# Modulation products moved from the softmax loop into the projection, head norm moved into the loop, recurrence norm split in two halves

## The reference, cut to what matters

```python
mod = silu(c) @ w_mod + b_mod                    # 6144 columns: six vectors of 1024
sh1, sc1, gt1, sh2, sc2, gt2 = split(mod, 6)
h = rmsnorm(x, g_pre_mix) * (1 + sc1) + sh1
parts = h @ w_in
# differential attention, 4 heads, 128 queries at a time
s = einsum(q, k_all) * scale                     # two maps m = 0, 1 of 1280 keys
pr = softmax(s)
o = (pr[0] - lam * pr[1]) @ v_all
y_d = rmsnorm(o, subln_w, 1e-5) * (1 - lam_init)     # over the 128 columns of a head
# recurrence
rw = dwconv(parts[..., :RWKV_COLS], rwkv_conv)
y = scan(forward) + scan(backward)
yn = (y - mean(y)) * rsqrt(var(y) + 64e-5) * ln_x_w + ln_x_b   # over the 64 columns of a head
y_r = (yn + bonus) * (sigmoid(gl) @ g2)
out = concat(y_r, y_d) @ w_out
x = x + gt1 * rmsnorm(out, g_post_mix)
h = rmsnorm(x, g_pre_ffn) * (1 + sc2) + sh2
```

## Time and profile before

| | us |
|---|---|
| median of 3 runs (3825.49 to 3829.32) | 3826.44 |
| the profiled execution | 3825.82 |
| its span (first to last instruction) | 3824.1 |
| TensorE busy in the span | 3526.0 (92%) |
| VectorE busy | 1891.0 (49%) |
| ScalarE busy | 936.4 (24%) |
| mean granted TensorE clock | 0.958 |

### The profile page before, as it was taken

The page is one execution under the profiler, slowest core; times in us unless marked ns, Lnnn a source line. Parts: engine busy times, 40 slices in busy tenths (PEclk is TensorE's granted clock), DMA queues, the critical chain, the costliest instruction groups (busy, mean ns, idle before and its releaser), DMA issues.

```text
span 3824.1 us, 63573 instructions
## 1 busy us (share of the span) xinstructions
PE 3526.0 (92%) x28813; PEld 2216.9 (58%) x28813; DVE 1891.0 (49%) x2735; ACT 936.4 (24%) x1856; POOL 47.2 (1%) x114
## 2 busy tenths in 40 slices
PE   7998879989999999498999989999899799999988
PEld 3446655559989888244444434445566445777753
DVE  2038852245555564435555550023999663444524
ACT  3015630125455554121000000000011301233310
POOL 2000000000000000000000000000000000000000
PEclk9999989989999999699999999999899899999999
DMA  6011110000000000213111121113011112010021
GB/s 224 22 44 67 67 66 7 28 6 18 4 17 4 4 4 6 94 55 105 66 61 44 42 77 41 50 55 94 22 33 39 39 67 62 22 34 23 1 81 62
DMA packets 110625, 177.53 MB, mean 46 GB/s; under 512 B 5379, under 2 KB 66562, under 8 KB 109714
## 3 DMA queue, kind: packets, MB, share of 16 engines
q1 hardware_dynamic: 101074, 139.49, 10.9%
q10 hardware_dynamic: 9280, 33.97, 2.4%
HBM read 147.23 MB, written 26.21 MB: 45 GB/s over the span
## 4 chain that ended last, share of the span: by engine, by line
PE 84%; DVE 9%; ACT 4%; DMA 2%; issue 1%; ACTq 0%; SPq 0%; DVEq 0%; POOL 0%; POOLq 0%
PE psum_all L66 82%; ACT sbuf_all L75 3%; DVE sbuf_all L94 3%; DVE sbuf_all L84 3%; DVE sbuf_all L102 3%; PE psum_all L69 2%; ACT L75 1%; DMA sbuf_all<-in_w_mod 1%; DMA sbuf_all<-in_w_out 1%; DVE sbuf_all L91 0%; DMA sbuf_all<-in_gla_w_out 0%; DVE sbuf_all L90 0%; DVE sbuf_all L108 0%; DMA sbuf_all<-in_w_down 0%; DVE sbuf_all L97 0%
## 5 line engine op out<-in xcount | busy, mean ns | idle before, releaser
L66 PE MATMUL psum_all<-sbuf_all 64*64 64x64 f32 (+11 forms) x28042 | 3419.2, 307 | 230.9 <-DVE sbuf_all L84 60.0
L66 PEld LDWEIGHTS psum_all<-sbuf_all 64*64 64x64 f32 (+5 forms) x28042 | 2124.9, 153 | 1503.5 <-issue 1066.0
L75 ACT ACTIVATE sbuf_all<-psum_all 128x512 f32<-128x512 f32 (+5 forms) x925 | 408.4, 461 | 1587.7 <-PE psum_all L66 1430.0
L94 DVE SCALAR_TENSOR_TENSOR sbuf_all<-sbuf_all 128x1040 f32<-128x1040 f32 (+8 forms) x571 | 624.1, 1094 | 24.8 <-PE psum_all L66 4.5
L84 DVE TENSOR_TENSOR sbuf_all<-sbuf_all 128x1024 f32<-128x1024 f32 (+9 forms) x589 | 469.7, 821 | 164.4 <-ACT sbuf_all L75 123.2
L75 ACT ACTIVATE sbuf_all<-sbuf_all 128x64 f32<-128x64 f32 (+12 forms) x449 | 259.9, 589 | 895.3 <-DVE sbuf_all L78 396.1
L78 DVE COPY sbuf_all<-psum_all 128x256 f32<-128x256 f32 (+5 forms) x137 | 71.2, 527 | 542.8 <-PE psum_all L66 529.0
L75 ACT ACTIVATE sbuf_all<-psum_all,sbuf_all 128x1280 f32<-128x1280 f32 (+5 forms) x212 | 164.3, 781 | 355.4 <-PE psum_all L66 325.1
L84 DVE TENSOR_TENSOR sbuf_all<-sbuf_all,psum_all 128x512 f32<-128x512 f32 (+3 forms) x160 | 102.0, 640 | 275.9 <-PE psum_all L66 274.8
L108 DVE COPY_PREDICATED sbuf_all<-sbuf_all,psum_all 128x256 f32<-128x256 int32 (+2 forms) x296 | 145.6, 493 | 159.0 <-PE psum_all L66 154.4
L69 PE MATMUL psum_all<-sbuf_all 128*128 128x128 f32 (+2 forms) x771 | 115.7, 295 | 55.9 <-DVE sbuf_all L90 27.1
(11 more groups left out here) (19 smaller groups left out, 125.7 us busy)
## 6 DMA issues: line engine op xcount, KB each, us to landing
sbuf_all<-in_w_mod SPq DMA_DIRECT2D x12, 2048.0 KB, 8.4
sbuf_all<-in_w_up SPq DMA_DIRECT2D x22, 1024.0 KB, 7.6
sbuf_all<-in_w_in SPq DMA_DIRECT2D x6, 2048.0 KB, 7.8
x_spill<-sbuf_all SPq DMA_DIRECT2D x16, 512.0 KB, 2.9
sbuf_all<-in_conv_w_in SPq DMA_DIRECT2D x16, 512.0 KB, 6.3
sbuf_all<-in_gla_w_in SPq DMA_DIRECT2D x8, 1024.0 KB, 5.3
sbuf_all<-in_w_down SPq DMA_DIRECT2D x4, 1792.0 KB, 7.5
hid_spill<-sbuf_all ACTq DMA_DIRECT2D x9, 512.0 KB, 2.6
```

The source lines that it names most:

```text
L66: return self.e.matmul(out, lhsT, rhs, start=start, stop=stop, skip_group_check=True)
L75: return self.e.activation(out, in_, func, bias=bias, scale=scale, **kw)
L94: return self.e.scalar_tensor_tensor(out, a, s, b, op0, op1) if self.e is not None else Unissued()
```

## The change

- The eight modulation blocks leave the softmax loop. In project, VectorE makes all eight products of one block after each of the first eight convolutions, into a `mod_acc` of its own, and TensorE sums each block a step later (steps 1 to 8), in a bank of the common ring. Project's weights use two slots (`rw_blocks`), the modulation one (`mod_blocks`), with the order of loads written out in `project_sync`.
- The norm and turning of head h move into the loop: turns 2 to 6 of the head after it, by the steps `head_mean`, `head_root`, `head_rows`, `turn_out`, `head_out`. Head 3 stays behind the loop.
- Lambda's matmul follows the first scores, and its exponential no longer holds the scores.
- Scanout is made by halves of positions (`scanout_norm`, `scanout_squares`, `scanout_turn`, `scanout_gated`). The second half is done inside mix: VectorE norms it after the gate row and the first half's gates; TensorE turns it ahead of the third block.
- `load_yd` and the `w_out` loads are issued from SP's queue, the first as soon as the scan ends, the others after the gate matmuls and GpSimd's product.

```diff
@@ softmax_tensor
+        if n == 0:
+            te.wait_ge(*A.v.by("lam_products"))
+            bank = open_bank(K, te, "lam", ring=K.small)
+            te.matmul(bank[:, 0:2], K.ones, K.lam[:, 0:2]).then_inc(*A.t.tick("lam"))
...
-        if n and n % 4 == 0 and n <= len(WORK):
-            mod_sum(3 + n // 4)
...
+        if n >= 12 and n % 8 in (4, 5):
+            turn_out(n // 8 - 1, n % 8 - 4)
+    for g in range(2):
+        turn_out(3, g)
@@ softmax_vector
         if n:
             combine(n - 1)
-        if n and n % 4 == 0:
-            mod_sum(3 + n // 4)
+        if h >= 0 and step in (5, 6):
+            head_out(h, step - 5)
         if n < len(WORK):
             top(n, 0)
             top(n, 1)
         if n:
             turned(n - 1, 8)
-        if n < len(WORK):
-            mod_rest(n)
+        if h >= 0 and step == 2:
+            head_mean(h)
+        if h >= 0 and step in (3, 4):
+            head_rows(h, step - 3)
+    head_mean(3)
+    for g in range(2):
+        head_rows(3, g)
+    for g in range(2):
+        head_out(3, g)
@@ softmax_scalar
+        if n >= 10 and n % 8 == 2:
+            head_root(n // 8 - 1)
+    head_root(3)
@@ project_tensor
+        if 1 <= n <= 8:
+            mod_sum(3 + n)
@@ project_vector
+        if 2 <= n <= 9:
+            mod_sum(2 + n)
+        if n < 8:
+            mod_products(4 + n)
@@ project_sync
+    inputs(("rw", 0), 0, RW)
+    inputs(("rw", 1), RW, RW)
+    for block in range(4, 8):
+        modulation(block)
+    inputs(("rw", 2), 2 * RW, RW)
+    for block in range(8, 12):
+        modulation(block)
+    inputs(("lowrank",), 3 * RW, 2 * LORA + GATE)
@@ mix_tensor
-    for s in K.scanout.ends():
-        te.wait_ge(*s)
     gate_row_tensor(K, te, M, "row1", K.mix_diag)
     te.wait_ge(*K.dma("load_yd").final())
     halves = [open_block(K, te, ("out", n), 512) for n in range(2)]
     for i in range(NT):
+        if i == 2:
+            scanout_turn(K, te, 1)
+        te.wait_ge(*K.scanout.v.by("gated", i // 4))
@@ mix_vector
-    for s in K.scanout.ends():
-        ve.wait_ge(*s)
+    ve.wait_ge(*K.scanout.t.by("gate", 1, 3))
     gate_row_vector(K, ve, M, "row1", K.mix_diag, K.mod[:, 16:24], K.col["g_post_mix"])
...
+    scanout_gated(K, ve, 0)
+    scanout_norm(K, ve, 1)
     for i in range(NT):
+        if i == 1:
+            scanout_gated(K, ve, 1)
@@ mix_scalar
+    gate_row_scalar(K, se, M, "row1", K.row1)
+    scanout_squares(K, se, 1)
@@ mix_sync
+    for s in (*K.scan.ends(), K.dma("spill_yd").final()):
         sy.wait_ge(*s)
+    sy.dma_start(K.ydT2, K.yd_dram).then_inc(*K.dma("load_yd").tick())
+    sy.wait_ge(*K.scanout.t.by("gate", 1, 3))
+    sy.wait_ge(*K.scanout.g.by("bonus"))
```

255 lines of the change are left out of this document (134 added, 121 removed).

## The result

The changed kernel takes 3776.28 us (median of 4 runs, 3774.14 to 3779.57), the kernel before 3825.97 (4 runs, 3824.03 to 3829.32): ratio 0.987, 95% interval 0.9853 to 0.9887, so 49.7 us less. Forecast were 3782.0 (3772 to 3792) and faster.

A forecast was written before the change was run, and what follows sets the result against it. Softmax keeps no engine full and is bound by a 7.10 us circle, project by TensorE, and the stretches behind loop and recurrence by serial chains. Terms -19.9 + 7.9 - 32.5 = -44.5 gave 3781.9 us, range 3772 to 3792.

The forecast's parts named there:

- rival 3: Mix starts with TensorE at full clock, giving 3.4 us more, 3778.5; with a cheaper loop 3771 to 3777, chance 0.08.
- Start of the loop: First softmax scores no longer wait for lambda's exponential and run warm: -3.8 us, bounds -2.0 and -4.2.
- Modulation out of the loop: Softmax loop: seven turns each lose the 1.29 us of the modulation sum, -9.0; the products were already covered, 0.
- Scaling of a turned group ahead of the maxima: Softmax loop, VectorE: a 0.78 us scaling between combine and maxima, 0.19 fitting into slack, six times 0.55: +3.3 us.
- Transposes in the loop: Softmax loop, TensorE: four transposes behind the weighing, mostly in idle time: +0.4 us, bounds 0 and +3.
- Root's table switch: Softmax loop, ScalarE: loading back the exponential's table behind the copies delays the second exponential, three times 1.15: +3.4 us.
- Rival 1: Softmax loop: each table switch costs ScalarE as much again as its 1.28 us load, +4.2, so 3786.1; chance 0.12.
- Behind the loop: After the softmax loop only head 3 is left, 5.5 us in place of 19.7: -14.2, bounds -13 and -15.
- Project: TensorE, the bound there, gets eight modulation sums of 0.98 us: +7.9, bounds +6 and +9; VectorE's products cost 0.
- rival 4: Project: one slot for modulation blocks starves it, slower kernel if a load takes 20 us or more; chance 0.02.
- Scanout: From recurrence's end to mix's first matmul: 34.0 us in place of 70.3, as mix needs only the first half: -36.3.
- Mix's first blocks: Turning the second half inside mix, warm, costs TensorE 3.8 us on top of cold-started blocks: +3.8.

The follow-up runs named there:

- modulation_back: The changed kernel with products and sums of the modulation in the softmax loop again, project as before: 3782.76 us.
- gate_row_in_gaps: The changed kernel with the gain row's blocks formed in VectorE's two waits inside the first half's norm, its matmuls ahead of the turning: 3774.75 us.
- products_later: The changed kernel with GpSimd's four products waiting for the first half's subtraction: 3779.11 us.
- scaling_on_scalar: The changed kernel with the last scaling of heads 0 to 2 on ScalarE, ahead of its copies, and not on VectorE: 3774.16 us.
- reload_early: The changed kernel with one single-column exponential right behind each of the three roots in the loop: 3767.91 us.
- heads_behind: The changed kernel with norm and turning of all four heads behind the loop again, with one root, modulation still in project: 3782.32 us.
- mix_as_before: The changed kernel with scanout and mix as in the kernel before: 3812.63 us.
- after_again: The changed kernel run once more, unchanged: 3778.50 us.
- lambda_first: The changed kernel with lambda's matmul and exponential ahead of the first scores again: 3781.88 us.
- squares_sooner: The changed kernel with GpSimd's products behind the subtraction and ScalarE's first-half squares ahead of its last four gate copies: 3778.28 us.

## Why the prediction was right, and where it was off

The sum was -44.5; the stages that the change touches gave -48.1, and each gain and cost came at the place that was named. The median of 3776.28 is inside the full range (3772 to 3792), but 0.7 below the stretch that had the chance of 0.63 (3777 to 3787), in the one given to rival 3 (3771 to 3777, 0.08); the second series' 3778.50 is inside the first. Part of that is luck of the clock, 3.2 us in the recurrence and 1.4 at the start of mix in the profiled execution. By its own terms:

- *Start of the loop*: -3.8 forecast, -4.8 to -4.9 measured, past the bound of -4.2. The first scores are warm, as taken (2.74), but the cold stretch behind them is shorter too: the third scores take 3.89 and not 4.64, and the steady turns begin 0.9 sooner for it. In three of twelve executions with this start (modulation_back, gate_row_in_gaps, products_later) the third scores are warm too and the gain is 7.2. The 2.74 hold lambda's two records; the scores alone are 2.42.
- *Modulation out of the loop*: -9.0 forecast and measured (seven turns of 8.39 to 7.11). That its products were covered holds; modulation_back shows where the cover would have run out (1.8 in three heads). With that and project's 7.5 the move is worth 3.4 of the whole.
- *Scaling of a turned group ahead of the maxima*: +3.3 forecast, 6 x 0.57 = +3.4 measured, and scaling_on_scalar shows that this is the whole cause. *Transposes in the loop*: +0.4 forecast, 0.
- *Root's table switch*: +3.4 forecast, 3 x 1.20 = +3.6. Rival 1 (each switch costs as much again) has fallen: in reload_early two loads stand 0.01 to 0.02 from their neighbours.
- *Behind the loop*: -14.2 forecast, 44.27 to 30.11 = -14.2 measured. In the prediction it came from "only head 3 is left"; heads_behind shows that 3.1 of it comes from counting by half heads.
- *Project*: +7.9 forecast, +7.5 measured. Steps of 18.08 with a sum and 17.09 without, products free, no wait for `w_mod`; rival 4 did not happen.
- *Scanout*: -36.3 forecast, -35.8 measured. The first half's norm took 22.5 against 22.1, turning 6.7 against 6.3 (bound 7; TensorE came to it from 15.4 us of idle time), what follows to mix's first matmul 5.3 against 5.6. "VectorE waits for the third only" was right: the subtraction ended at 8.0, against 8.1, and GpSimd's fourth product waited for it. Scale and subtraction lost 3.1 us in all, and products_later shows that without it the squares would have stood behind ScalarE's copies nearly as long.
- *Mix's first blocks*: +3.8 forecast, +1.0 measured, the term that was furthest off in the compared pair: "its turning is then all that it costs" was put on top of "two cold-started blocks of mix". The turning does cost its 3.8 (four banks at 0.93 each), but mix started warm and gave 2.8 back. That is rival 3, with a chance of 0.08. It came about in four of nine executions with this order. In two more the term was +2.7 and in three +3.9, the forecast's own size; there the turning had been quicker, and mix started up to 1.5 sooner by it. With scanout taken in, the forecast of -32.5 stands against -34.8 in the four and -33.3 in the five: 2.3 or 0.8 off. Turning with the gain row's first two, and the four blocks, in modulation_back, where the changed kernel has 7.73 and 59.25:

```profile
1532.94 6.24 PE L66 MATMUL psum_all<-sbuf_all 64*64 64x64 f32 x130 [15.43 <-DVE sbuf_all L84]
1543.46 62.17 PE L66 MATMUL psum_all<-sbuf_all 128*128 128x512 f32 x256 [1.55 <-DVE sbuf_all L84]
```

  The counter-argument to rival 3 was the gain row's matmul, cold after 2.44 us of idle time behind the turning. Now 1.61 us lie ahead of it and 1.55 ahead of mix, and the row's second matmul took 1.12, where its first had taken 2.05. mix_as_before shows the slow start with the old order.
- *Recurrence*: 0 forecast, -3.2 in the profiled pair: a clock that differs between executions of the same code, which no term of the sum could have held.

Terms missed: start of the loop -1.1, project -0.4, mix's start -2.8 on the one side, scanout +0.5 on the other, which is the 3.6 between -44.5 and -48.1; the few tenths left are the transposes that cost nothing, the table switch, and stages ahead of softmax that ended 0.3 later.

## What to carry to other kernels

When a serial tail is split so that its first part releases the next stage, the gain is the tail less the first part, and an engine that comes straight from work may also save its cold start (here in four of nine executions), so give that a chance and not a place in the sum. Ahead of reading a difference of 3 us from two traces, look whether the granted clock of the same stretch differs. A load of ScalarE's table costs its 1.28 us where it stands in the queue: force the load back (one small exponential) into idle time, and put a scaling on the engine that idles at that point. If taking a collision away changes nothing, look at what the next instruction waits for now (the idle time before it and its releaser), since a second chain of nearly the same length was hidden behind the first.

## What the hardware did that I had not expected

- TensorE's granted clock falls in the recurrence in the same 20 us of all fourteen executions, but by different amounts: to a mean of 0.74 in nine and 0.91 in five, with 308 or 376 matmuls done in it, although TensorE is at work nearly all the time. This makes steps of some 3.3 us between executions.
- The start of mix differs likewise between executions, behind 1.5 to 1.7 us of idle time. Its first 10 us were at 1.00 in four (the changed kernel, heads_behind, reload_early, products_later), at 0.83 in two (after_again, lambda_first) and at 0.70 to 0.71 in three (modulation_back, scaling_on_scalar, squares_sooner), as slow as the old order's 0.69 and 0.70. After_again's:

```profile
1544.08:1554.08 10.00, 10.00 (x20) 4.35 (x21) 7.59 (x7) 2.14 (x2) 0.00 (x0) 0.83 0.01 2
```

  The quicker the turning ahead of it (6.5 to 6.7, 6.4, and 5.2 to 5.5 us), the longer the four blocks (66.8, 68.5 and 69.8 us): the full clock came sooner in the turning and fell again as mix began. What sets which of the three comes is left open.
- The first turns of the softmax loop came in two ways, 25.3 to 25.4 us for three in nine of the executions with the new start and 23.0 in three, behind the same 0.8 us of idle time.
- One product of GpSimd can hold up a VectorE instruction on 32 columns: the scaling of the mean took 1.65 us beside it and 0.18 without. The reduction beside the first product took 2.29 with and without it.
